# Triangular inverse by levels: products, copies and masks on 32 columns instead of 64

## What is computed

```python
def step(state, inp):
    r_t, w_t, k_t, v_t, al_t, be_t = inp
    sa = jnp.einsum("bhvk,bhk->bhv", state, al_t)
    state = (state * w_t[:, :, None, :] + sa[..., None] * be_t[:, :, None, :]
             + v_t[..., None] * k_t[:, :, None, :])
    return state, jnp.einsum("bhvk,bhk->bhv", state, r_t)
```

## Time and profile before

| | before |
|---|---|
| median of 3 runs | 4411.39 us (4407.91 to 4414.4) |
| profiled execution | 4417.7 us, of which the span of the trace is 4415.9 us |
| TensorE products | 3578.9 us busy, 81% of the span |
| TensorE weight loads | 2198.1 us, 50% |
| VectorE | 1958.7 us, 44% |
| ScalarE | 1338.6 us, 30% |
| GpSimd | 1513.0 us, 34% |
| mean granted clock of TensorE | 0.903 |

### The profile page before, as it was taken

One profiled execution on the slowest core, in us unless ns is written; L12 is line 12 of the kernel. 1 busy time (PEld: TensorE's weight loads), 2 busy tenths in 40 slices (PEclk: granted clock), 3 DMA queues, 4 the chain that ended last, 5 costly groups with the idle time before them and its releaser, 6 DMA issues. The chain is left out here.

```text
span 4415.9 us, 76666 instructions
## 1 busy us (share of the span) xinstructions
PE 3578.9 (81%) x32170; PEld 2198.1 (50%) x32170; DVE 1958.7 (44%) x2375; ACT 1338.6 (30%) x1919; POOL 1513.0 (34%) x791
## 2 busy tenths in 40 slices
PE   4876887868857897598898788888888788887888
PEld 2333565644423343488887345554543355545533
DVE  2463657561244456555454344442341244444341
ACT  3233434341244422233233333331210233332211
POOL 2443333333523454233332412223254322222353
PEclk7988898988968998799999889989999799999999
DMA  4101100002122444311111101102011011110011
GB/s 157 39 24 41 29 28 24 28 5 86 33 86 57 96 99 105 101 53 53 40 52 39 65 20 38 46 10 62 10 60 53 30 29 28 38 47 25 29 60 52
DMA packets 308717, 218.34 MB, mean 49 GB/s; under 512 B 125459, under 2 KB 284126, under 8 KB 306398
## 3 DMA queue, kind: packets, MB, share of 16 engines
q1 hardware_dynamic: 308482, 214.80, 16.7%
HBM read 173.07 MB, written 41.71 MB: 49 GB/s over the span
## 5 line engine op out<-in xcount | busy, mean ns | idle before, releaser
L126 PE MATMUL psum<-u,w_hi 128*128 128x512 f16 x3584 | 1088.0, 386 | 178.1 <-DVEq L447 43.7
L97 POOL TENSOR_TENSOR w_hi<-stage,w_scale 128x1024 f16<-128x1024 f32 x200 | 396.1, 1980 | 2292.6 <-PE psum L126 1231.3
L126 PE MATMUL psum<-u,w_lo 128*128 128x512 f16 x1792 | 689.3, 385 | 0.0
L126 PEld LDWEIGHTS psum<-u,w_hi 128*128 128x128 f16 x3584 | 353.1, 99 | 625.9 <-issue 119.6
L101 POOL TENSOR_TENSOR w_lo<-stage,w_hi 128x1024 f16<-128x1024 f32 x200 | 489.0, 2445 | 28.5
L943 PE MATMUL psum<-w_hi,merged 128*128 128x512 f16 x1536 | 463.8, 383 | 26.0 <-ACTq L966 16.2
L99 POOL TENSOR_TENSOR stage<-stage,w_scale 128x1024 f32<-128x1024 f32 x200 | 423.7, 2119 | 28.6
L943 PE MATMUL psum<-w_lo,merged 128*128 128x512 f16 x768 | 294.5, 383 | 0.0
L126 PEld LDWEIGHTS psum<-u,w_lo 128*128 128x128 f16 x1792 | 177.8, 99 | 219.5 <-issue 14.3
L141 PE MATMUL psum<-w_hi,u 128*128 128x128 f16 x3072 | 266.2, 222 | 0.0
L141 PE MATMUL psum<-w_lo,u 128*128 128x128 f16 x1536 | 264.1, 221 | 0.0
(11 more groups left out here) (410 smaller groups left out, 6100.3 us busy)
## 6 DMA issues: line engine op xcount, KB each, us to landing
stage<-w_in SPq DMA_DIRECT2D x72, 512.0 KB, 6.0
rwkv_chunks<-work_rp SPq DMA_DIRECT2D x56, 512.0 KB, 3.9
X<-rwkv_chunks SPq DMA_DIRECT2D x16, 1792.0 KB, 8.0
stage<-ab_w_in SPq DMA_DIRECT2D x48, 512.0 KB, 3.9
stage<-rw_w_in SPq DMA_DIRECT2D x32, 512.0 KB, 6.5
stage<-w_out SPq DMA_DIRECT2D x24, 512.0 KB, 6.3
X<-x SPq DMA_DIRECT2D x16, 512.0 KB, 8.0
stage<-ab_w_out SPq DMA_DIRECT2D x16, 512.0 KB, 3.5
```

What stands on the lines that cost most here:

```text
L97: pool.tensor_tensor(K.w_hi[:, slot, :], K.stage[:, slot, :], scale, ALU.mult)
L126: last = pe.matmul(K.psum[:, bank, :], w[:, k, :], u[:, k, cols], start=(k == 0 and n == 0), stop=(k == KT - 1 and n == 2))
```

## The change

Per level, work is confined to the 32 columns (of 64) that the level changes. `side(x, lv, 1)` picks the later block of each couple, `side(x, lv, 0)` the earlier one, as a strided view in runs of 1, 2, 4, 8, 16 or 32 columns. The moving operand of each level product is such a view; the weights are whole as before. The result lies packed in PSUM (32 columns for each pair). ScalarE's copy writes the changed columns of Y only, and Y is set to zero once at the start of the stage (on VectorE). The masked copies write the 32 columns of Tt or T with a mask of 32 columns, and the table of masks is half as large. The number of instructions is as before, but for that one memset.

```diff
-        tmask = sb("tmask", [P, 2, len(LEVELS), RW_C], U32)
+        tmask = sb("tmask", [P, 2, len(LEVELS), RW_C // 2], U32)
...
-        half = lambda n, h: K.psum[:, n, h * GJ * RW_C:(h + 1) * GJ * RW_C].rearrange("p (j t) -> p j t", j=GJ)
+        HW = RW_C // 2
+        half = lambda n, h: K.psum[:, n, h * GJ * HW:(h + 1) * GJ * HW].rearrange("p (j t) -> p j t", j=GJ)
...
+        def blocks(x, lv):
+            return x.rearrange("p j (n b) -> p j n b", b=LEVELS[lv])
+        def side(x, lv, later):
+            return x.rearrange("p j (n a b) -> p j n a b", a=2, b=LEVELS[lv])[:, :, :, later, :]
...
-                            last = pe.matmul(half(Y_BANK + g, 0)[hp, j % GJ], N[hp, j, :], Tt[hp, q, j, :],
-                                             start=True, stop=True)
+                            last = pe.matmul(blocks(half(Y_BANK + g, 0), lv + 1)[hp, j % GJ], N[hp, j, :],
+                                             side(Tt[:, q], lv + 1, 1)[hp, j], start=True, stop=True)
...
-                            last = pe.matmul(half(Z_BANK + g, 0)[hp, j % GJ], T[hp, q, j, :], Y[hp, j, :],
-                                             start=True, stop=True)
+                            last = pe.matmul(blocks(half(Z_BANK + g, 0), lv + 1)[hp, j % GJ], T[hp, q, j, :],
+                                             side(Y, lv + 1, 1)[hp, j], start=True, stop=True)
...
-                                last = pe.matmul(half(Z_BANK + g, 1)[hp, j % GJ], Y[hp, j, :], T[hp, q, j, :],
-                                                 start=True, stop=True)
+                                last = pe.matmul(blocks(half(Z_BANK + g, 1), lv + 1)[hp, j % GJ], Y[hp, j, :],
+                                                 side(T[:, q], lv + 1, 0)[hp, j], start=True, stop=True)
...
-                        act.copy(Y[:, g * GJ:g * GJ + GJ], half(Y_BANK + g, 0)).then_inc(y_ready, 1)
+                        act.copy(side(Y[:, g * GJ:g * GJ + GJ], lv + 1, 1),
+                                 blocks(half(Y_BANK + g, 0), lv + 1)).then_inc(y_ready, 1)
...
+                dve.memset(Y, 0.0)
...
-                        grow_turned(0, g, q, pairs(0)[:, g * GJ:g * GJ + GJ, 0, :])
+                        grow_turned(0, g, q, side(pairs(0)[:, g * GJ:g * GJ + GJ, 0, :], 0, 1))
...
-                        grow_plain(0, g, q, N[:, g * GJ:g * GJ + GJ])
+                        grow_plain(0, g, q, side(N[:, g * GJ:g * GJ + GJ], 0, 0))
...
-                    mask = tmask[:, 0, lv:lv + 1, :].broadcast_to([P, GJ, RW_C])
-                    dve.copy_predicated(Tt[:, q, g * GJ:g * GJ + GJ], mask, data).then_inc(t_ready, 1)
+                    mask = blocks(tmask[:, 0, lv:lv + 1, :], lv).broadcast_to([P, GJ, HW // LEVELS[lv], LEVELS[lv]])
+                    dve.copy_predicated(side(Tt[:, q, g * GJ:g * GJ + GJ], lv, 1), mask, data).then_inc(t_ready, 1)
```

More of the change, by code:

```diff
@@ L1861, in grow_turned @@
                 def grow_turned(lv, g, q, data):
-                    mask = tmask[:, 0, lv:lv + 1, :].broadcast_to([P, GJ, RW_C])
-                    dve.copy_predicated(Tt[:, q, g * GJ:g * GJ + GJ], mask, data).then_inc(t_ready, 1)
+                    mask = blocks(tmask[:, 0, lv:lv + 1, :], lv).broadcast_to([P, GJ, HW // LEVELS[lv], LEVELS[lv]])
+                    dve.copy_predicated(side(Tt[:, q, g * GJ:g * GJ + GJ], lv, 1), mask, data).then_inc(t_ready, 1)
                 def grow_plain(lv, g, q, data):
-                    mask = tmask[:, 1, lv:lv + 1, :].broadcast_to([P, GJ, RW_C])
-                    dve.copy_predicated(T[:, q, g * GJ:g * GJ + GJ], mask, data).then_inc(plain_ready, 1)
+                    mask = blocks(tmask[:, 1, lv:lv + 1, :], lv).broadcast_to([P, GJ, HW // LEVELS[lv], LEVELS[lv]])
+                    dve.copy_predicated(side(T[:, q, g * GJ:g * GJ + GJ], lv, 0), mask, data).then_inc(plain_ready, 1)
                 def grow(c, q, lv):
@@ L1872, in grow @@
                         held(dve, z_done, c * P_STEPS + (2 * lv + g + 1))
-                        grow_turned(lv + 1, g, q, half(Z_BANK + g, 0))
+                        grow_turned(lv + 1, g, q, blocks(half(Z_BANK + g, 0), lv + 1))
                         if lv + 1 < NL:
-                            grow_plain(lv + 1, g, q, half(Z_BANK + g, 1))
+                            grow_plain(lv + 1, g, q, blocks(half(Z_BANK + g, 1), lv + 1))
                 def body(ch, p, inverse, finish, following):
@@ L2729, in constants @@
     levels = (1, 2, 4, 8, 16, 32)
-    grown = [(i // (2 * b) == k // (2 * b)) & (i // b % 2 == 0) & (k // b % 2 == 1) for b in levels]
-    turned = [(i // (2 * b) == k // (2 * b)) & (k // b % 2 == 0) & (i // b % 2 == 1) for b in levels]
+    later = lambda b: (lambda c: 2 * b * (c // b) + b + c % b)(np.arange(RW_C // 2))[None, :]
+    grown = [(i // (2 * b) == later(b) // (2 * b)) & (i // b % 2 == 0) for b in levels]
+    turned = [(i // (2 * b) == later(b) // (2 * b)) & (i // b % 2 == 1) for b in levels]
     rel = np.arange(REL) - (S - 1)
```

## The result

| | before | changed |
|---|---|---|
| median time | 4410.5 us (4407.91 to 4414.4, 4 runs) | 4459.05 us (4457.81 to 4463.2, 4 runs) |
| ratio | | 1.0107, 95% interval 1.0094 to 1.012 |
| profiled execution | 4417.7 us, span 4415.9 | 4463.2 us, span 4461.4 |
| mean granted clock of TensorE | 0.903 | 0.886 |
| stage, first instruction to last | 623.8 us | 671.2 us |

The change makes the kernel slower by 48.5 us, outside the range of the prediction (4387 to 4430). Between the two profiled executions the difference is 45.5 us, and the stage alone is 47.4 us longer, so all of it lies there. The last two rows of the table are sums over the records of the trace; some 18 us of the half-clock time lie ahead of the stage's first product, in both kernels.

A forecast was written before the change was run, and what follows sets the result against it. TensorE was taken to set the pace. Shorter waits 8.0, faster products 4.9 and entry 0.5 us, together 13.4 us off the 4411.4 us median, gave 4398.0 us; the range was 4387 to 4430.

The forecast's parts named there:

- the term of the clock: TensorE's clock during the level products: the sum charged nothing for a fall, which was left to the first rival.
- the first rival: In levels 2 to 4, half the columns plus the stop lower TensorE's clock: price 31.8 us, 4430 us; chance 0.25.
- The pace of the products: Steps of the stage's level products, 58.2 ns before, get slightly shorter: 4.9 us saved, bounds 0 to 16 us.
- lockstep: Lower bound for the level products' steps: load, start of product and next load stay as before, 0 us saved.
- The waits: TensorE's waits for VectorE's and ScalarE's copies in levels 2 to 4 get shorter: 8.0 us saved.
- the shorter last product: A group's last product, with 32 columns, lasts some 25 ns less in each of the waits for copies.
- The entry: At the stage's start the mask table's halved DMA lets the first chunk's load come earlier: 0.5 us saved.
- The stops: Where TensorE waits for its own instructions, standstills grow and swallow gains: 7.2 us left, 4404 us; chance 0.24.
- The columns case: Moving columns, not weight loads, set the level products' step: 83 us saved there, 4320 us; chance 0.08.
- What would show it: Trace signs: masked copies near 310 ns, ScalarE's near 266, level products near 195, waits 0.31 and 0.18 us.
- The sign given for the clock: Trace sign of the first rival: granted clock under 1.00 in levels 2 to 4, L1599 longer.

The follow-up runs named there:

- e1: Changed kernel with the level products back on all 64 columns, copies and masks still on 32; 4410.33 us, 0.9991 of before.
- the burst with 16 moving columns: Kernel before plus unread bursts of 64 identity products at the stage's entry, here 64 weight columns and 16 moving; the execution with all bursts took 4436.16 us.
- e6: Changed kernel plus three unread products of 128x256 columns in each chunk, right ahead of level 3; 4450.55 us, 1.0087 of before.
- e3: Changed kernel with each level product streaming its broken 32-column view twice, the second result unread; 4408.46 us, 0.9986 of before.
- e5_wide_late: Changed kernel with products of levels 2 to 4 on 64 columns, those of the first two levels on 32; 4410.42 us, 0.9992 of before.

## Why the prediction was wrong, point by point

**The step that failed is the term of the clock: nothing in the sum that gave 4398.0, and too small a price in the rival.** The sum took every level product at full clock, as before. The mechanism was in the prediction as the first rival, with the right place (levels 2 to 4, behind the stop; eleven of the falls lie behind one, ten of them in levels 2 and 3), but at a chance of 0.25 and a price of 31.8 us; the runs show 69.5 us of slower steps (below), and 4459.05 us lies 29 over the rival's 4430. The one argument against it was that the clock stays up over the stop in the kernel before; with all columns it does, with half of them it doesn't, and the row could not speak for that. Two things were missing from the price:

- The level products themselves. Against e1 they are busy 44.2 us longer (339.6 less 295.4), the largest part. The prediction doubled only L1599's pair and L1498's burst. These two cost 28.4 - 18.0 = 10.4 and 47.6 - 36.7 = 10.9 us, 21.3 together, less than the 31.8 put down for them. The level products were left out since their loads were taken as the bound, and a load's time as fixed. It isn't: at full clock sixteen records are 0.465 us apart, at half clock 0.85 (2157.47 to 2158.32), with loads of up to 228 ns instead of 135.
- How long it lasts. The price let the low clock take one pair or one burst. It took 224 us of the stage, up to 24 us at a stretch and 27 in the last chunk. Behind the fall the steps are narrow products too, and in none of them did the clock come back: each time it came back in the first products of the next chunk, with 128 and 64 columns each (L1507, L1513), and in the last chunk, which has no such products behind it, only in the outputs (2454.3).

Counted over all records of the changed kernel from 1819 us on that ran at half clock: 1893 level products at 24.2 ns more each, 45.8 us (steps of 106.7 instead of 58.3 ns, two records a step); 356 products of 128 columns at 52 ns, 18.5; 25 of 512 columns at 0.478 us, 12.0; 264 others of 64 columns at 24.2 ns, 6.4. Together 82.7 us, against 13.2 in the kernel before (163 records of 128 columns, 4 of 512 and 117 of 64): 69.5 more. The stage grew by 47.4. Of the 22 between, 15 are waits: what TensorE's records of the stage start later than a step behind the one before them, where it is over 0.2 us, comes to 57 us instead of 72. The last 7 us I can't place.

The rule that the prediction cited for its step of the loads, the Trainium skill (TensorE: Matmul & The Clock Gate, "LDWEIGHTS (loading the stationary operand)"), gives 53 ns for 64 columns without a word on the array's clock. The 58.3 ns a step at full clock lie 5 over that; the 106.7 at half clock don't fit, and the measurement decides. The other that it cited, the Trainium skill on the clock (same page, "What's actually happening"), has it follow how busy the array has been. Here it followed the columns streamed at the same number of instructions, which no sentence there rules out: the burst with 16 moving columns shows it with the engine never idle.

**The pace of the products**, 4.9 us, was mis-sized: it is nothing. The range was 0 to 16 us by loads of 53 to 56 ns, and I took half of the 9.8 that 55 ns give; steps stay at 58.3 ns with 64, 32 or 16 moving columns. The loads bind exactly, the end called "lockstep". The 55 ns came of two rounded lengths (0.19 less 0.133), which leave 52 to 62: taken one by one, the first load of L1498 starts at 2065.608 and the third at 2065.667, 59 ns behind, so the trace of before had held the answer. In the trace of the changed kernel too sixteen narrow records are 0.465 us apart (2054.36 to 2054.82), as in the earlier trace rows.

**The waits**, 8.0 us, are seen in e1, where the clock doesn't hide them. The masked copy takes 300 ns (310 forecast), ScalarE's 266 to 269 (266). The start of a Y half behind the other came 0.13 us earlier (gaps of median 0.47 to 0.34 us), Z behind Y 0.11 (0.32 to 0.21): 24 x 0.13 + 32 x 0.11 = 6.6 us. The rest of the 8.0, 56 x 0.025 = 1.4 us, was the shorter last product, and that term is nothing: at full clock a record of 32 columns lasts 219 ns (median) where 195 were forecast and 64 columns have 218, and in the changed kernel a Y half starts 0.34 us behind the other and Z 0.20 behind Y, as in e1 (0.34 and 0.21). The entry's 0.5 us can't be told from noise.

**The stops**, the second rival, were partly right. They stay where they are in the program, whatever runs there: counted in TensorE's records from the loop round's first product they lie at 740 and 1600 in each of five rounds of before and of e1 (at times with a third, at 618 or 1480), and at 740 or 618 and at 1600 in the changed kernel. In e6, where the added products shift the program, they lie at 728 (in all rounds but one) and 1588. They are 0.7 to 1.7 us long. Inside and behind Z's products they come to 20.5 us before and to 22.0, 24.5 and 23.0 in e1, e3 and e5_wide_late: of the 6.6 us won, part went into them, and 4 to 6 us are what e1 and e3 measure against before. These sums are each of one execution, so how large that part is stays open. With 4404 for what is left, that rival would have been the nearest to these kernels. That a stop is TensorE waiting for its own instructions is argued from its place only; no run here showed it.

**The columns case** (4320) is out by the bursts: 32 moving columns pass in 58.3 ns a step with 64 loaded, in 31.9 with 32 loaded.

**What would show it** was right for the copies (300 ns for 310, 266 for 266), the loads' 135 ns, the distances (0.465 us) and the 1.28 us, and wrong for the level products (219 ns for 195) and with them the waits (0.34 and 0.20 us for 0.31 and 0.18). The sign given for the clock, a granted clock under 1.00 in levels 2 to 4 with a longer L1599 (L1608 in the changed kernel), is what the trace showed.

## What to carry to other kernels

Before you halve the moving columns of small products, find out what spaces them: where each loads its own weights of as many columns, the narrower product comes no earlier, and it may take away the work that keeps TensorE's clock up. Narrow the copies and masks and leave the products wide (e1_wide_products, 0.9991 of before, 0.9981 to 1.0): that is the form that is not slower here. Streaming the narrow view twice (e3_streamed_twice, 0.9986) does as well. Both gains are under 0.2%, so the change is hardly worth making for its own sake. And when a fall of the clock is one of the rivals, price every record behind it until something wide comes, its loads included, and not the one wide product next to it.

## What the runs showed of the hardware

- A 64-column load of f32 holds the next one back for 58.3 ns at full clock and 106.7 at half: loads slow down with the clock, and a narrow product at half clock is as slow as a wide one.
- With 32 loaded and 32 moving columns a step is 31.9 ns, with 32 and 64 it is 55.9: at 64 by 64, load and stream are nearly equal, so only halving both brings time.
- The clock fell under a TensorE without a gap (64 loaded, 16 moving columns), seen once (0.50 right behind that burst); behind an equal burst with 32 moving columns it stayed at 1.00. Where narrow products are mixed with wide ones (levels 0 and 1 of e5_wide_late, 0.96 to 0.98 a loop round) it held.
- More work cost no time: with 34.4 us of unread products the changed kernel's median is 4450.55 us instead of 4459.05 (overlapping intervals), with 123 us at half clock instead of 224.
- Broken views in runs of 2 to 32 columns cost nothing on the moving side of these products, whose loads take as long as 64 columns (e3_streamed_twice 4408.46 us, e1_wide_products 4410.33).
